# A rotary step in a two-block kernel: who swaps the 32-row halves, and from where

## The reference

```
def apply_rope(t, cos, sin):
    half = t.shape[-1] // 2
    t1, t2 = tf[..., :half], tf[..., half:]
    return jnp.concatenate([t1 * c - t2 * s, t2 * c + t1 * s], axis=-1)

    qa = apply_rope(parts[0].reshape(B, S, 2 * DA_HEADS, DA_HEAD_DIM), cos, sin)
    ka = apply_rope(parts[1].reshape(B, S, 2 * DA_HEADS, DA_HEAD_DIM), cos, sin)
    ...
        qg = apply_rope(parts[base].reshape(B, S, DB_HEADS, DB_HEAD_DIM), cos, sin)
        kg = apply_rope(parts[base + 1].reshape(B, S, DB_HEADS, DB_HEAD_DIM), cos, sin)
```

## Time and profile before

| | |
|---|---|
| median of 3 runs | 4309.51 us (4307.07 to 4314.01) |
| profiled execution, its own time | 4309.57 us |
| its span | 4307.8 us |
| mean granted TensorE clock | 0.937 |
| first layer's stage of 48 chunks | about 2314 to 2724 us of the span |
| second layer's | about 3324 to 3735 us |

### The profile page before, as it was taken

How to read it: one execution, slowest core, us unless ns; L and a number is a source line. 1 busy time by engine, 2 the same in 40 slices (tenths; PEclk the granted TensorE clock), 3 DMA queues, 4 the chain that set the end, 5 groups by cost and what they waited for, 6 DMA issues and landing times.

```text
span 4307.8 us, 56019 instructions
## 1 busy us (share of the span) xinstructions
PE 3926.6 (91%) x20866; PEld 3122.1 (72%) x20866; DVE 1735.6 (40%) x2756; ACT 1537.7 (36%) x2554; POOL 1432.9 (33%) x644
## 2 busy tenths in 40 slices
PE   6947888999998799999997999989997999998998
PEld 4844556788886577778885777867885777886886
DVE  2784432524242455534434655232113556332112
ACT  3312224412123444433325555333223555424222
POOL 2569103222222100024442323334443223342443
PEclk9966778999999899999998999999998999999999
DMA  4313432111111000023231222222222112221222
GB/s 176 123 53 117 147 113 79 49 64 64 59 64 64 30 20 19 15 68 103 94 102 60 69 64 69 81 71 88 98 94 68 64 60 72 76 96 61 98 98 83
DMA packets 84551, 332.58 MB, mean 77 GB/s; under 512 B 9505, under 2 KB 9761, under 8 KB 77857
## 3 DMA queue, kind: packets, MB, share of 16 engines
q1 hardware_dynamic: 83664, 328.18, 22.7%
q10 hardware_dynamic: 720, 2.10, 0.1%
HBM read 328.14 MB, written 2.10 MB: 77 GB/s over the span
## 4 chain that ended last, share of the span: by engine, by line
PE 64%; issue 22%; POOL 8%; DVE 3%; ACT 2%; POOLq 0%; DVEq 0%; ACTq 0%
PE pB L281 12%; PE pB L282 12%; PE pB L283 12%; PE pB L1579 12%; POOL w_lo L2099 4%; POOL under L1040 2%; PE pO L1194 2%; PE pS L394 2%; POOL under L1042 2%; PE pB L1176 1%; PE pT L1186 1%; PE pS L1176 1%; PE pS L1609 1%; PE pT L1637 1%; PE pO L1659 1%
## 5 line engine op out<-in xcount | busy, mean ns | idle before, releaser
L2099 POOL TENSOR_TENSOR w_lo<-w_raw,w_hi 128x1024 fp32r<-128x1024 f32 x518 | 1256.5, 2427 | 2806.0 <-ACT w_hi L319 2805.7
L281 PE MATMUL pB<-h_hi,w_hi 128*128 128x512 f32 x2072 | 817.3, 394 | 56.6 <-POOL w_lo L2099 25.4
L282 PE MATMUL pB<-h_lo,w_hi 128*128 128x512 f32 x2072 | 814.1, 393 | 0.0
L283 PE MATMUL pB<-h_hi,w_lo 128*128 128x512 f32 x2072 | 813.1, 392 | 0.0
L319 ACT ACTIVATE w_hi<-w_raw 128x1024 fp32r<-128x1024 f32 x518 | 546.8, 1056 | 615.3 <-PE pB L283 406.3
L281 PEld LDWEIGHTS pB<-h_hi,w_hi 128*128 128x128 f32 x2072 | 395.2, 191 | 145.9 <-issue 50.8
L283 PEld LDWEIGHTS pB<-h_hi,w_lo 128*128 128x128 f32 x2072 | 394.5, 190 | 83.1
L282 PEld LDWEIGHTS pB<-h_lo,w_hi 128*128 128x128 f32 x2072 | 395.1, 191 | 80.1
L281 PE MATMUL pB<-b_hi,w_hi 128*128 128x512 f32 (+1 forms) x1112 | 410.4, 369 | 16.4 <-DVE xb_lo L646 10.6
L282 PE MATMUL pB<-b_lo,w_hi 128*128 128x512 f32 (+1 forms) x1112 | 408.8, 368 | 0.0
L283 PE MATMUL pB<-b_hi,w_lo 128*128 128x512 f32 (+1 forms) x1112 | 408.4, 367 | 0.0
(11 more groups left out here) (399 smaller groups left out, 5756.6 us busy)
## 6 DMA issues: line engine op xcount, KB each, us to landing
w_raw<-stream SPq DMA_DIRECT2D x518, 512.0 KB, 3.3
under<-ada SPq DMA_DIRECT2D x42, 1024.0 KB, 4.9
arena<-ada SPq DMA_DIRECT2D x6, 1024.0 KB, 17.1
x<-xT SPq DMA_DIRECT2D x1, 2048.0 KB, 8.8
out<-x SPq DMA_DIRECT2D x8, 256.0 KB, 2.0
xc<-cT SPq DMA_DIRECT2D x1, 1024.0 KB, 9.9
arena<-bmask ACTq DMA_DIRECT2D x1, 1024.0 KB, 4.8
arena<-brope ACTq DMA_DIRECT2D x2, 256.0 KB, 5.2
```

The lines of the kernel that those rows point to most:

```text
L281: pe.matmul(dst, lh, rh, start=(begin and k == 0), stop=False)
L282: pe.matmul(dst, lh, rl, start=False, stop=False)
L283: last = pe.matmul(dst, ll, rh, start=False, stop=(end and k == len(pairs) - 1))
L2099: pool.tensor_tensor(w_lo[:, s, :], w_raw[:, s, :], w_hi[:, s, :].bitcast(F32), ALU.subtract).then_inc(lo_ready, 1)
```

## The change

The four crosswise copies on ScalarE are left out, and with them the semaphore `swapped`. VectorE waits for the chunk itself, and multiplies each 32-row block of the bank with the same rows of the sines, writing the product to the block that is its partner. The sign of the sines is turned over, since they now lie by the source row and not by the destination row. The multiply of `qsw` by the sines on 128 rows is gone, and with it the semaphore `rope_step`; the addition now waits on the count that the cosine multiply raises. ScalarE keeps its wait for the chunk and its conversion of the next weights.

```
@@ act_chunk
             elif kind(k)[0] != "v":
-                r = l * N_ROPES + ROPE_NO[k]
-                if r >= 2:
-                    act.wait_ge(rope_done, r - 1)
-                for q in range(0, P, 64):
-                    for a, b in ((q, q + 32), (q + 32, q)):
-                        last = act.activation(qsw[r % 2][a:a + 32, :], bank[s][b:b + 32, :], ACT.Copy)
-                last.then_inc(swapped, 1)
+                pass
@@ dve_rope
-            dve.wait_ge(swapped, r + 1)
+            dve.wait_ge(chunk_done, done(G_DIFF[l] + k))
+            if r >= 2:
+                dve.wait_ge(rope_done, r - 1)
+            for q in range(0, P, 64):
+                for a, b in ((q, q + 32), (q + 32, q)):
+                    dve.tensor_tensor(qsw[r % 2][a:a + 32, :], bank[s][b:b + 32, :], sin2[b:b + 32, :], ALU.mult)
             dve.tensor_tensor(to, bank[s][:, :], cos2, ALU.mult).then_inc(evac[s], 1)
-            dve.tensor_tensor(qsw[r % 2], qsw[r % 2], sin2, ALU.mult).then_inc(rope_step, 1)
-            dve.wait_ge(rope_step, r + 1)
             dve.wait_ge(*ev(G_DIFF[l] + k))
@@ shape_constants
-    sign = np.where(np.arange(P) % 64 < 32, -1.0, 1.0)[:, None]
+    sign = np.where(np.arange(P) % 64 < 32, 1.0, -1.0)[:, None]
```

More of the change, by code:

```diff
@@ L1566, in program @@
         pair_ca, pair_cd, pair_v, pair_o = sem("pair_ca"), sem("pair_cd"), sem("pair_v"), sem("pair_o")
-        swapped, rope_step, vfm_ready, gates_ready = sem("swapped"), sem("rope_step"), sem("vfm_ready"), sem("gates_ready")
+        vfm_ready, gates_ready = sem("vfm_ready"), sem("gates_ready")
         def pe_products(pe, l, a, b):
```

## The result

The changed kernel takes 4324.42 us in the median of 12 runs (4319.7 to 4332.47), the kernel before 4309.72 in 12 runs taken with it (4306.54 to 4316.38): ratio 1.0035, interval 1.0026 to 1.0044. It is slower by 0.35%, 14.7 us. The forecast of 4315.0 us had the sign of the balance right and the size short: 5 us more where 15 came. The measured time lies inside the range of 4295 to 4327, but not in the 4303 to 4318 of the first case, and by the forecast's own limit of 0.2% it is slower (given 32%), not the same (48%).

What follows compares the result with a forecast made beforehand. TensorE, busy 91%, was taken as the bound, so only its waits near rotary steps count. The kernel before's 4309.6 us plus 6.8 for waits less 1.4 for clock gave 4315.0 us, range 4295 to 4327.

Steps and rivals of the forecast that it cites:

- the first case: Likeliest outcome: the gains and losses of waits and clock balance as summed, 4303 to 4318 us, 46%.
- the four places named: Where TensorE is near the rotary steps: the start of a layer, Place A, Place B and Place C.
- Place C: Even turns, third pass, four a layer: two back-to-back steps, both additions blocked by GpSimd, next scores wait: +2.17 us each.
- Place B: Odd turns but the last, last pass, three a layer: TensorE's 1.3 us wait for L1877 goes, -4.0 us.
- Place A: Odd turns but the last, third pass, three a layer: output L1890 comes later, TensorE waits 0.42 us each, +1.3.
- Start: Start of a layer, once: the first two rotary steps end sooner, so the first scores start 2.6 us earlier.
- Sum of waits: All four kinds of places together, without the clock: +3.4 us a layer, +6.8 us.
- Clock: Low-clock stretches of 1.7 us behind two or three Place C waits, the start's loss halved: -1.4 us in all.
- Rival 2: Each new wait at Place C drops the clock, 4323 us, or Place A too, 4333 us; 32%.
- Rivals 3 and 4: 3: Place C does not come, 4289 us, 17% including clock staying up; 4: all hidden, start included, 4309 to 4311, 5%.

Runs made afterwards that it cites:

- e2: The changed kernel with all four narrow multiplies reading and writing rows 0 to 31, swap left out: 4309.48 us beside 4310.48 for the kernel before.
- e1: The changed kernel with ScalarE converting the next weights at a rotary chunk only after the previous rotary step: 4296.87 us beside 4310.48 for the kernel before.
- e5: The changed kernel with outputs written between the narrow multiplies and the cosine multiply in odd turns' second pass: 4329.24 us beside 4312.92 for the kernel before.
- b2: The kernel before with weight conversions ahead of the copies, and two at each layer's start only after the second rotary step: 4289.68 us, ratio 0.9963.
- e6: The changed kernel with the weight conversion at each layer's third chunk only after the second rotary step: 4314.75 us beside 4312.92 for the kernel before.
- e9: e7 with each layer's second rotary step in the old form (ScalarE copies) and b2's conversions at the start: 4274.13 us, ratio 0.9919 to the kernel before.
- e7: The changed kernel with the edits of e1 (from each layer's fourth chunk on), e5 and e6 together: 4290.14 us, ratio 0.9950 to the kernel before.

## Why the prediction was right, and where it was short

- *The mechanism stood.* TensorE moved only at the four places named; 77 us a layer less on ScalarE brought nothing. All else of both engines stayed hidden.
- *Place C*: forecast +2.17 us four times a layer, by two additions each caught by a subtraction; measured +2.02, eight times (by the forecast's own times, 2477.3 less 2475.16, it was +2.14). The blocked additions took 1.69 and 1.82 us and not up to 2.4, since they were ready later; their ends stayed. That the multiply's price doesn't move this end was right too (e2: 2.0 with the cheaper multiply). e1 shows that it is the lock.
- *Place B*: forecast -4.0 a layer, measured -3.95.
- *Place A*: forecast +1.3 a layer, measured 3 x 0.84 = +2.5. The term that was mis-sized is the multiply: 0.605 us from start to start was taken from two wide operations on the same rows. At 0.70, with 0.1 more before the first, it is 0.5 us a step. The forecast named another time than 0.6 us as a sign that it was wrong, and in this term it was.
- *Start*: forecast -2.6, measured +0.14. It is the same 0.1 us. The forecast said "addition ready at 2321.3" against a subtraction that "can't start before 2321.9": a margin of 0.6 us. From the first multiply of a step to its addition it took 3.53 us and not 3.1, twice 0.4; 0.2 came back, as the first addition was no longer blocked. What was left, between 0.6 and 0.7 us, used the margin up. The range of the multiply's price, 0.59 to 0.69, ended just short of the true value. At its upper end the margin would have shrunk to 0.1 or 0.2 us. I didn't run it through, and so missed that the gain of 2.6 us hung on it.
- *Sum of waits*: +3.4 a layer forecast, +6.8 measured, 2.7 from the start and 1.2 from A, less 0.6 at C. Two layers: 13.7 us.
- *Clock*: two to three falls at C a layer were forecast and two came; the start's were to halve and stayed whole. -1.4 forecast, about 0 measured.
- *Rival 2*, all falls at C and 4323 us, met the time but not the way: in the changed kernel two of four fell. In e5 all four do. The measured time lies inside the range because the range takes in this rival; against the sum itself, three times as much was lost as forecast. That part is luck. Rivals 3 and 4 are out, as place C came.
- The lower bound came from ScalarE's copies of the same shape. The engines differ in just this: on ScalarE the blocks changed as well and the copies follow each other at 0.60.

What stays open is why the clock falls behind one wait of 2.0 us and not behind the next one like it. In e5 a gain of 5 us in waits is gone again in the time, with more low stretches in the trace, and no experiment here sets them.

## What to carry to other kernels

When work moves from one engine to another, look at what the engine left behind will now start earlier, and whom that meets: here the weight conversion and GpSimd's subtraction behind it. Run both ends of an unknown price through every margin of the plan, not only through the sum: a price of 0.60 or 0.70 us decided 15 us. And look for the lock between VectorE and GpSimd in the spread of one line's durations before moving any work: reordering ScalarE's list alone, with the step left as it was (b2), gained 18 us, where moving the copies alone had cost 15.

## What the runs showed of the hardware

- VectorE on another block of 32 rows than the instruction before: 0.70 us from start to start, on the same block 0.60, for 512 columns; width and crossing don't matter.
- A VectorE addition of 128x512 with two SBUF operands ends 0.55 us behind GpSimd's subtraction when it comes second, even by 0.04 us. Bank-reading multiplies, 256 of them, took 679 to 698 ns whatever GpSimd did, and held no subtraction up: one that began during them took its 2.36 to 2.41 us.
- A TensorE wait of 1.3 us can be followed by a stretch of low clock worth 1.7 us, and one of 2.0 us can go without. Halving or removing waits at the start of a stage gave back two to three times their length (e6: 4.3 us of waits, 9.7 of time against the changed kernel; e9 against e7: 4.9 and, by the ratios, 13).
